# Head norms of a fused decoder layer: one norm per head, or four heads in one norm

## The reference

```
q, k, v = silu(causal_conv(h @ w_in[q|k|v]))      # 4 heads x 128 channels each
q, k    = l2norm(q), l2norm(k)                    # x * rsqrt(sum(x*x over the head) + 1e-6)
o       = gated_delta_chunked(q * 128**-0.5, k, v, g, beta)
...
kk      = l2norm((kc * rwkv_k_k) by head)         # 4 heads x 64 channels
```

## Time and profile before

| | us |
|---|---|
| median of 3 runs | 1339.4 (1336.93 to 1343.01) |
| the profiled execution | 1342.74 |
| its span, first to last instruction | 1341.0 |
| TensorE busy in the span | 1236.7 (92%) |
| ACT, DVE, POOL busy | 360.4, 466.8, 526.6 |

### The profile page before, as it was taken

How to read it: one execution, slowest core, us unless ns; L and a number is a source line. 1 busy time by engine, 2 the same in 40 slices (tenths; PEclk the granted TensorE clock), 3 DMA queues, 4 the chain that set the end, 5 groups by cost and what they waited for, 6 DMA issues and landing times. The chain is left out here.

```text
span 1341.0 us, 30955 instructions
## 1 busy us (share of the span) xinstructions
PE 1236.7 (92%) x12565; PEld 848.1 (63%) x12565; DVE 466.8 (35%) x1137; ACT 360.4 (27%) x836; POOL 526.6 (39%) x785
## 2 busy tenths in 40 slices
PE   6999999999989898999985999986999999999990
PEld 6666666665656567787863455454777777777770
DVE  3124543442276713546442102143222222222223
ACT  4003112333353323555631222220111111111114
POOL 7000000030182035787833020104666666666662
PEclk9899999999989998999996999988999999999996
DMA  7111111121203110000027410349999999799737
GB/s 197 27 37 33 33 32 33 47 48 31 55 16 82 37 39 13 22 17 22 13 66 235 143 64 32 126 123 332 349 311 372 309 312 353 242 314 353 252 56 274
DMA packets 138695, 182.73 MB, mean 136 GB/s; under 512 B 37120, under 2 KB 85751, under 8 KB 138602
## 3 DMA queue, kind: packets, MB, share of 16 engines
q1 hardware_dynamic: 122472, 160.61, 35.6%
q0 software_dynamic: 15936, 20.57, 7.4%
q10 hardware_dynamic: 194, 0.23, 0.1%
HBM read 152.09 MB, written 29.28 MB: 135 GB/s over the span
## 5 line engine op out<-in xcount | busy, mean ns | idle before, releaser
L426 PE MATMUL ps<-hT,w_in 128*128 128x352 f32 (+1 forms) x1296 | 402.0, 469 | 0.8 <-DVE conv_state_T L872 0.8
L426 PEld LDWEIGHTS ps<-hT,w_in 128*128 128x128 f32 x1296 | 249.1, 193 | 141.8 <-issue 9.0
L2775 POOL DMA_INDIRECT sum_rows<-slot_out,scatter_rows x76 | 121.6, 1600 | 38.6 <-POOL scatter_rows L2774 26.2
L2814 PE MATMUL ps<-qkv,slot_T 128*32 128x256 f32 x1920 | 111.4, 383 | 9.0 <-DVE slot_T L2901 8.2
L2901 DVE TENSOR_TENSOR slot_T<-slot_raw_T,vecs 128x256 f32<-128x256 f32 x75 | 32.4, 432 | 214.3 <-PE ps L2814 214.3
L2814 PEld LDWEIGHTS ps<-qkv,slot_T 128*32 128x32 f32 x1920 | 75.6, 111 | 38.6 <-issue 9.8
L2752 POOL DMA_INDIRECT gathered<-h_rows,gather_rows x79 | 83.6, 1058 | 20.6 <-issue 12.5
L2858 ACT ACTIVATE slot_silu<-ps 128x128 f32<-128x128 f32 x77 | 21.5, 279 | 225.9 <-PE ps L2814 223.6
L2814 PE MATMUL ps<-cb,slot_T 128*32 128x256 f32 x1408 | 80.6, 379 | 0.0
L2814 PEld LDWEIGHTS ps<-cb,slot_T 128*32 128x32 f32 x1408 | 55.4, 110 | 20.5
L2027 PE MATMUL ps<-qkv,zg 128*128 128x512 f32 (+1 forms) x144 | 67.5, 612 | 0.0
(11 more groups left out here) (645 smaller groups left out, 2063.7 us busy)
## 6 DMA issues: line engine op xcount, KB each, us to landing
w_in<-in_w_in SPq DMA_DIRECT2D x28, 512.0 KB, 4.0
qkv<-in_expert_w_gate SPq DMA_DIRECT2D x6, 2048.0 KB
qkv<-in_expert_w_up SPq DMA_DIRECT2D x6, 2048.0 KB
qkv<-in_expert_w_down SPq DMA_DIRECT2D x6, 2048.0 KB, 19.5
cb<-in_expert_w_gate SPq DMA_DIRECT2D x5, 2048.0 KB
cb<-in_expert_w_up SPq DMA_DIRECT2D x5, 2048.0 KB
zg<-in_expert_w_down SPq DMA_DIRECT2D x5, 2048.0 KB
third_w_down<-in_expert_w_down SPq DMA_DIRECT2D x5, 2048.0 KB, 16.2
```

The costliest lines, as they stand in the source:

```text
L426: last = pe.matmul(pbank(b)[:, c, 0:n], w[:, k, :], hT[:, k, c * CH:c * CH + n], start=(k == 0), stop=(k == KD - 1))
L2775: pool.indirect_dma_start(quarter_sums, bass.IndirectOffsetOnAxis(ap=sidx[:, r:r + 1], axis=0), y[r][:], None, compute_op=ALU.add).then_in ...
L2814: last = pe.matmul(gu_bank[c4[c], 0:2 * QF].rearrange("p (x b d) -> p x b d", x=2, d=32), xT[:, k, :], of_quarter(by_block[u][k], c), star ...
```

## The change

Norms are regrouped. The four k heads form norm 0, the four q heads norm 1 (`heads_of`), and the two halves of kk stay single as norms 2 and 3. For a norm of four heads:

- ACT squares the four heads into four separate buffers (`spread`, parts of lw, bb and cb that are free then). The squares are put after the Silu of blocks q8 and q9.
- TensorE multiplies each head's squares by 32 columns of ones only, in four column groups: head i gives partitions 32i to 32i+31 of one bank.
- ACT takes one logarithm and one exponential for the four heads, into acc[n] (zg blocks 2 and 3).
- SP writes the four rows, one per head, to memory (norm_rows), waits, and reads each back into all 128 partitions of the head's spread buffer (64 counts of rs_in per norm). It also waits for the first norm's reads before it issues those of the second.
- DVE multiplies each head by its spread buffer.

The single norms of kk come right behind, with rs in acc[1]. The table of steps moves everything ahead, from c2 on, with nothing left beside c0, c1, z0 and z1. `near_grams_a` goes from the third chunk of c7 to the second of c6, and `to_instances("A")` on SP from behind the weights of c0 to behind those of c7. Three semaphores are folded into others (hp, zeroed, counts of vec).

```diff
-        norms = [4, 5, 6, 7, None, None, 0, 1, 2, 3]
+        heads_of = [range(4, 8), range(4)]
+        spread = [[lw[:, 0], lw[:, 1], bb[:, 0], bb[:, 1]], [cb[:, 0], cb[:, 1], cb[:, 4], cb[:, 5]]]
@@ SP
+                def norms_by_head(n):
+                    sp.wait_ge(s.rs, n + 1)
+                    sp.dma_start(norm_rows[n], acc[n][0:P:32, :]).then_inc(s.rs_out, 16)
+                    sp.wait_ge(s.rs_out, 16 * (n + 1))
+                    sp.wait_ge(s.rs_in, 16 * H * n)
+                    for i in range(H):
+                        sp.dma_start(spread[n][i], norm_rows[n, i].partition_broadcast(P)).then_inc(s.rs_in, 16)
@@ SP, in the loop over weights, each after load_w(j)
-                    if b == "c0":
+                    if b == "c3":
+                        norms_by_head(0)
+                    if b == "c6":
+                        norms_by_head(1)
+                    if b == "c7":
                         to_instances("A", 1, LcA, invA)
@@ TensorE
-                        pe.matmul(ps[:, 6 + (n + c) % 2, 0:CH], lhs[:], sq[:, c * CH:c * CH + CH], start=True, stop=True).then_inc(s.nrm, 1)
+                    if n < 2:
+                        for i, r in enumerate(BLOCKS):
+                            last = pe.matmul(ps[r, b, 0:CH], m.ones[:, 0:32], spread[n][i][:, x], start=True, stop=True)
+                    else:
+                        last = pe.matmul(ps[:, b, 0:CH], m.blk64[:], sq[:, x], start=True, stop=True)
@@
                 def near_grams_a():
                     pe.wait_ge(s.nrm_done, 4)
-                    pe.wait_ge(s.nrm_ln, 3 * 4)
+                    pe.wait_ge(s.nrm_ln, 3 * 3)
@@
-                steps = {("c3", 0): [part(0, 0, 1)], ("c3", 1): [part(0, 2)], ("c3", 2): [part(1, 0, 1)],
-                         ("c6", 0): [part(1, 2)], ("c6", 1): [part(2, 0, 1)], ("c6", 2): [part(2, 2)],
-                         ("c7", 0): [part(3, 0, 1)], ("c7", 1): [part(3, 2)], ("c7", 2): [near_grams_a],
-                         ("c0", 0): [part(4, 0, 1)], ("c0", 1): [part(4, 2)], ("c0", 2): [part(5, 0, 1)],
-                         ("c1", 0): [part(5, 2)], ("c1", 1): [part(6, 0, 1)], ("c1", 2): [part(6, 2)],
+                steps = {("c2", 0): [part(0, 0, 1)], ("c2", 1): [part(0, 2)], ("c2", 2): [part(1, 0, 1)], ("c3", 0): [part(1, 2)],
+                         ("c3", 2): [part(2, 0, 1)], ("c6", 0): [part(2, 2)], ("c6", 1): [near_grams_a], ("c6", 2): [part(3, 0, 1)],
+                         ("c7", 0): [part(3, 2)],
                          ("c4", 0): [near_grams_c(0), near_grams_c(1)], ("c4", 1): [near_grams_c(2), near_grams_c(3)],
-                         ("c4", 2): [near_grams_c(4), near_grams_c(5)], ("c5", 0): [near_grams_c(6), near_grams_c(7)],
-                         ("c5", 1): [part(7, 0, 1)], ("c5", 2): [part(7, 2)],
-                         ("z0", 0): [part(8, 0, 1)], ("z0", 1): [part(8, 2)], ("z0", 2): [part(9, 0, 1)], ("z1", 0): [part(9, 2)]}
+                         ("c4", 2): [near_grams_c(4), near_grams_c(5)], ("c5", 0): [near_grams_c(6), near_grams_c(7)]}
@@ ACT
+                def squares(n):
+                    ...
+                    for i, j in enumerate(heads_of[n]):
+                        last = act.activation(spread[n][i], qkv[:, j, :], ACT.Square)
+                    last.then_inc(s.sq, 1)
+                def square(c):
+                    act.wait_ge(s.kr, c + 1)
+                    act.wait_ge(s.rs_out, 32)
+                    act.activation(sq, kk[c], ACT.Square).then_inc(s.sq, 1)
@@
+                    if j in (8, 9):
+                        squares(j - 8)
@@ ACT, after block q11
                 act.preload_act_table_set(LNEXP)
                 act.drain()
-                square(0)
                 act.wait_ge(s.decay, 1)
                 act.activation(decA[:], decA[:], ACT.Exp).then_inc(s.near_exp, 1)
+                norm_logs(0, 0, 1, 2)
+                norm_exp(0)
+                norm_logs(1, 0, 1)
                 out_shift(2)
-                norm(0)
-                square(1)
+                norm_logs(1, 2)
+                norm_exp(1)
+                square(0)
+                norm_logs(2, 0, 1)
                 out_shift(3)
                 ...
+                norm_logs(2, 2)
+                norm_exp(2)
+                square(1)
+                norm_logs(3, 0, 1)
                 out_shift(6)
-                norm(3)
-                square(4)
+                norm_logs(3, 2)
+                norm_exp(3)
                 out_shift(7)
-                norm(4)
-                square(5)
@@ DVE
                 def normed(n):
+                    dve.wait_ge(s.rs_in, 64 * (n + 1))
+                    for i, j in enumerate(heads_of[n]):
+                        dve.scalar_tensor_tensor(qkv[:, j, :], qkv[:, j, :], HA ** -0.5 if j < 4 else 1.0, spread[n][i],
+                                                 ALU.mult, ALU.mult).then_inc(s.nrm_done, 1)
@@
                 shifted(2)
                 removal_key(0)
                 normed(0)
+                normed(1)
                 shifted(3)
                 removal_key(1)
-                normed(1)
-                normed(2)
+                normed_key(0)
+                near_a()
                 shifted(6)
-                normed(3)
-                near_a()
+                normed_key(1)
                 shifted(7)
-                normed(4)
```

More of the change, by code:

```diff
@@ L55 @@
 NROWS = _at
-SEMS = """ident masks wgz sguS rows cs sw small samp_w x0 x1 x2 x3 x4 x5 x6 x7 x8 rstd dg xT hT vec setupT hp zeroed sgT sgTd shT shc shift_out
+SEMS = """ident masks wgz sguS rows cs sw small samp_w x0 x1 x2 x3 x4 x5 x6 x7 x8 rstd dg xT hT vec setupT sgT sgTd shT shc shift_out rs_out rs_in
 w0 w1 pj ev vT vc var vr vn mix vout rows_out conv silu tails out_c sq nrm nrm_ln rs nrm_done mixd drv kr kc gate_pe gate_act gate_dve gco bk zt zte
@@ L486, in _ @@
                     scaled_tile(i)
-                pe.wait_ge(s.vec, 1)
+                pe.wait_ge(s.vec, 2)
                 pe.wait_ge(s.cs, 32)
@@ L565, in part @@
                 def part(n, *cs):
-                    go = norm_chunk(n, m.ones if norms[n] is not None else m.blk64)
                     def parts():
                         if n == 0 and cs[0] == 0:
-                            pe.wait_ge(s.gate_act, GATE_ACT["decays"])
                             pe.wait_ge(s.gate_act, GATE_ACT["rows"])
-                        if n == 4 and cs[0] == 0:
+                        if n == 3 and cs[0] == 0:
                             pe.wait_ge(s.near_read, 1)
-                        if n == 7 and cs[0] == 0:
-                            pe.wait_ge(s.near_read, 2)
                         for c in cs:
-                            go(c)
+                            norm_chunk(n, c)
                     return parts
@@ L700, in out_shift, with norm_exp @@
                                    pbank(b)[:, 2, SEQ - 2 * CH:CH].rearrange("p (b t) -> p b t", t=TB), ACT.Copy).then_inc(s.ev, 1)
-                def square(n):
-                    j = norms[n]
-                    if j is None:
-                        act.wait_ge(s.kr, n - 3)
-                    act.activation(sq, kk[n - 4] if j is None else qkv[:, j, :], ACT.Square).then_inc(s.sq, 1)
+                def squares(n):
+                    act.wait_ge(s.shift_out, 32)
+                    act.wait_ge(s.rows_out, 16)
+                    act.wait_ge(s.vout, 3)
+                    for i, j in enumerate(heads_of[n]):
[5 more added lines that the diff above has]
+                    act.activation(sq, kk[c], ACT.Square).then_inc(s.sq, 1)
                 def norm_logs(n, *cs):
-                    if n >= 1:
-                        act.wait_ge(s.nrm_done, n)
+                    dst = acc[n] if n < 2 else rs
+                    if n == 3:
+                        act.wait_ge(s.nrm_done, 9)
                     for c in cs:
                         act.wait_ge(s.nrm, 3 * n + c + 1)
-                        act.activation(rs[:, c * CH:c * CH + CH], ps[:, 6 + (n + c) % 2, 0:CH], ACT.Ln, bias=L2_EPS).then_inc(s.nrm_ln, 1)
-                def norm_exp():
+                        act.activation(dst[:, c * CH:c * CH + CH], ps[:, 6 + (n + c) % 2, 0:CH], ACT.Ln, bias=L2_EPS).then_inc(s.nrm_ln, 1)
+                def norm_exp(n):
+                    dst = acc[n] if n < 2 else rs
                     act.drain()
-                    act.activation(rs, rs, ACT.Exp, scale=-0.5).then_inc(s.rs, 1)
-                def norm(n):
-                    norm_logs(n, 0, 1, 2)
-                    norm_exp()
+                    act.activation(dst, dst, ACT.Exp, scale=-0.5).then_inc(s.rs, 1)
                 def early_exps(e):
@@ L792, in _ @@
                 out_shift(0)
[L793 removed]
+                act.wait_ge(s.nrm_done, 4)
                 for j in range(2):
@@ L801, in _ @@
                 act.preload_act_table_set(LNEXP)
-                norm(5)
-                square(6)
-                norm_logs(6, 0, 1)
```

(16 more changed lines are left out.)

45 lines of the change are left out of this document (15 added, 30 removed).

## The result

| | median us | lowest to highest | runs |
|---|---|---|---|
| before | 1341.65 | 1336.93 to 1345.30 | 6 |
| after | 1327.53 | 1326.49 to 1329.73 | 6 |

The ratio after to before is 0.9899, 95% interval 0.9883 to 0.9914: 14.1 us faster by the medians. The forecast was 1322.7 us, range 1316 to 1334. Of the 4.8 us between, 2.6 are gain that did not come (14.1 where 16.7 were forecast); the other 2.2 are the base: the median of the first three runs of before was 1339.4, that of six is 1341.65.

What follows compares the result with a forecast made beforehand. TensorE, busy 92% of the span, was taken to bound the kernel. Removing 25.8 us and adding 9.1 us gave 16.7 us off 1339.4, so 1322.7 us, range 1316 to 1334.

Steps and rivals of the forecast that it cites:

- (a): Norm work on TensorE: four-head passes in column groups cut 17.9 us to 7.4, 10.5 us less.
- (b): TensorE's wait at 314 us in c6 for a norm's logarithm, with low clock behind it, goes: 3.8 us.
- (d): TensorE's wait at 459.92 us in z1 for a norm's logarithm, with low clock, goes: 5.8 us.
- (c): Wait at 383.85 us before c1, with low clock, shrinks to 1.1 us for l4's eviction: 5.2 us gained.
- (e): TensorE's 1.1 us wait for the early keys, half counted as gained: 0.5 us.
- new wait: TensorE waits before c2's second chunk, at norm 0's third chunk, for ACT's logarithm: 7.1 us added.
- low clock behind it: The granted clock falls after TensorE's wait at c2: 2.0 us added, bounds 0 to 3.5.
- changes of tiling: Eight TensorE drains around four column-group places: charged nothing, with 1.3 us named as an estimate.
- Transfers: Each norm's four replicating reads take 8 us, covered by slack, so they cost TensorE nothing.
- R1: Rival: slow replicating reads make TensorE wait at c6's third chunk; slower at 1348 or partial gain at 1332; 15 in 100.
- The tie: z1's eviction ends at 473.9 us, nearly when TensorE's transposes need it, 1.8 us after z2; hidden by one or two us.
- R2: Rival: DVE's near-C chain holds z1's eviction and the first tile; gain near 12 us, 1327 us; 20 in 100.

Runs made afterwards that it cites:

- e3: Changed kernel with each chunk of the two four-head norms computed four times: 1332.43 us, ratio 0.9949 to the kernel before.
- e2: Changed kernel with chunk 1 of norm 0 computed ten times, filling the new wait: 1323.84 us, ratio 0.9882 to the kernel before.
- e1: Changed kernel with four-head norm steps later on TensorE, first logarithms earlier on ACT, normed(1) behind near_a: 1318.53 us, ratio 0.9829 to before.
- e4: Changed kernel with each set of four replicating reads done three times in sequence: 1353.27 us, ratio 1.0096 to the kernel before.
- e5: Changed kernel with near_grams_a halved ahead of c6's second and third chunks, norm 3 one step later: 1325.19 us, ratio 0.9883 to before.
- e7: Changed kernel with 18 extra small matmuls (36 products) ahead of norm 0's first chunk: 1325.98 us, ratio 0.9893 to the kernel before.
- e9: Changed kernel with 64 extra small matmuls (128 products) ahead of norm 0's first chunk: 1327.96 us, ratio 0.9905 to the kernel before.
- e8: Kernel before with 46 extra small matmuls (92 products) ahead of norm 0's first chunk: 1345.08 us, ratio 1.0037 to the kernel before.
- e6: Changed kernel with the edits of e1 and e5 together: 1316.45 us, ratio 0.9815 to the kernel before.

## Why the prediction was right, and the step that failed

The mechanism, the place of the new wait and the direction were right. By its own terms, in the profiled executions:

| term | forecast | measured |
|---|---|---|
| (a) passes | -10.5 | -10.2 |
| (b), (d) waits for norms in c6, z1 | -9.6 | gone, -9.6 |
| (c) c1 | -5.2, 1.1 stays | -5.5, 1.2 stays |
| (e) early keys | -0.5 | wait gone, -1.1 |
| new wait | +7.1 | +6.7 |
| low clock behind it | +2.0 | +2.3 |
| changes of tiling, in the chunks beside | 0 | +0.6 |
| pause in the gram burst | not there | +1.5 |
| low clock behind that | not there | +1.7 |
| sum | -16.7 | -13.6; the stage shows -13.3 |

The measured column counts only rows, except that the low clock in (b) and (d) is the forecast's. For (d) the rows bear it out: the six chunks from 460.59 to z2's end at 490.89 take 30.30 us in before, and after's twelve from 417.57 to 474.90 take 57.33, so 28.67 for six. For (c) the forecast read 0.5 too little: start to start, before's norm chunk at 383.85 takes 1.31 us in place of 0.59 and the projection chunk behind it (385.16 to 391.97) 6.81 in place of 4.73, so 2.8 us of low clock and not 2.3. The four places with column groups take 1.32, 0.73, 1.32 and 0.73 us at full clock, 4.1 in all, so (a) is 17.9 - 4.1 - 3.6. The 0.3 us left in the last row is not assigned.

**Passes.** Four column groups did run beside each other (e3: 0.592 us a pass). The rule of the Trainium skill on changes of tiling (TensorEngine Tiling (Array Packing), Key Properties) agrees with the trace: a place costs 0.34 us, 1.3 to 1.4 us for four. In after 0.55 of it stand in the norm rows and 0.6 in the chunks beside; the entry of the first place lies ahead of the stage and that of the second inside the wait. The forecast charged nothing because it saw no gap beside the gate columns at 201 us; the price is no gap but a longer chunk. The 1.3 us that it had as an estimate by the Trainium skill's figure was the right one.

**The new wait.** The chain Silu of q11, table load, exponential of near_decay_A, logarithm was the right one. It ran 3 us earlier with the whole front. e2 separates idle time from clock; e1 takes both away and gains 9.0 us, what the two measured rows make together (forecast 9.1).

**Transfers.** Forecast 8 us a set, measured 9.1 in after and 9.0 apart in e4. Norm 1 waited 3.95 us on DVE and still cost TensorE nothing, as the forecast said. R1 was a real mechanism with too few places (e4).

**The tie.** R2 would have ended at 1327, the time measured, but it did not happen: z1's eviction ended at 474.69 (forecast 473.9), and TensorE asks for it after 476. A right total for R2 would have been no proof of it; only the row decides.

**The step that failed** is above all one that the working lacks: I took every instruction that neither waits nor changes to keep its duration. near_grams_a did not; its pause grew from 0.37 to 1.90 us because the number of instructions ahead of it changed, and the clock fell behind it. e5 and e7 (stage 3.5 and 3.9 us shorter), e9 (no effect for a whole block) and e8 (the loss carried over to the old kernel) show that. With it, 16.7 becomes 13.5, inside the interval measured, 11.5 to 15.7 us. The second step is "I charge nothing" for the changes of tiling (1.1 us of the price fell into the stage; 0.2 of it the forecast had in its 0.63 us a pass). That it does not show in the sum is luck: (c) and (e) gave 0.9 us more than forecast and the wait was 0.4 shorter, against 0.3 more for the clock behind it.

## To carry to other kernels

When one norm serves many heads, pack them in column groups of one pass: the pass costs the same, and going into the groups and back is 0.34 us. Then look not at what was removed but at where the first new step waits: an order change that costs nothing gave 9 us more than the packed norms alone. And treat a dense burst of tiny TensorE products as sensitive to its position in the stream: keep it to 128 at a stretch with long instructions between, and check it in the trace after every edit ahead of it.

## What the runs showed of the hardware that was not expected

**Pauses inside a burst at every 256 instructions of TensorE.** The trace also records the transfers that bring instructions: queue q8, 68 of them and 1.11 MB in after, so 16 KB each, or 64 bytes for each of 256 instructions. Each stop in the burst has one shortly before it. The one in after, alone in the window from 328.2 to 328.4 us:

```profile
DMA packets 1, 0.02 MB, mean 82 GB/s; under 512 B 0, under 2 KB 0, under 8 KB 0
q8 instruction: 1, 0.02, 29.2%
```

The place within the burst, the length of the pause, when the transfer began against the first of the two boundaries, and the time from its start to TensorE's next product behind the second:

| boundary after product | pause us | kernel | transfer begins | from its start to the next product |
|---|---|---|---|---|
| 12, 140 | none | e7 | 2.7 us ahead | |
| 13, 141 | 0.37 at 141 | before | 0.75 ahead | 2.40 |
| 32, 160 | 1.78 at 160 | e3 | 0.7 behind | 2.37 |
| 48, 176 | 1.90, 2.22, 2.42, 2.20 at 176 | after, e9, e1, e4 | 0.8 to 1.0 behind | 2.38, 2.60, 2.66, 2.50 |
| 49, 177 | 1.96 at 177 | e8 | 0.9 behind | 2.35 |
| 104, 232 | 2.08 at 232 | e2 | 1.0 behind | 2.36 |

It is always the second boundary of the burst that stops. In all eight kernels that stop, TensorE goes on 2.35 to 2.66 us after the transfer of 16 KB began (which itself takes 0.9 to 1.3 us), whatever the place and the length of the pause. A block of 128 products is used up in 1.1 to 1.3 us there, and in some 38 us among projection products (4.73/16 us each). So a transfer that begins 0.7 us or more behind the first boundary is late at the second, and one that begins 2.7 us ahead of it (e7) is not; in e5 and e6 it begins 1.0 and 0.8 us behind it, but the second boundary lies over 6 us behind the first. By these rows the pause is the wait for the next block of instructions. Why the transfer begins ahead of a boundary at 12 or 13 products and behind one at 32 stays open.

**Low clock behind short stops comes and goes.** Behind waits of 5.4 to 6.8 us the next projection chunk was slow each time (6.6 to 6.95 us, five kernels); behind the 9.7 and 13.2 us of e4 two norm chunks took 2.51 us start to start in place of 1.18, and the projection chunk behind them 6.07 and 5.67. Behind 1.97 us it was slow in before (6.13) and not in e8 (4.90); behind the gram pause of 1.8 to 2.4 us it was slow in after, e1, e8 and e9 and not in e2, e3 and e4; behind 3.25 us in e3 it was not (5.00). The granted clock in the 2 us behind the gram pause was 0.50 in e1, 0.55 in e9 and 0.61 in e8, and 1.00 in e2. A stop of 2 to 3 us is thus a chance of 1.0 to 1.8 us more, not a fixed price. Work that is thrown away, put into the wait of 6.7 us, was a gain of some 2 us in the trace (e2).
